# Attention over keys in multiples of 64, and top-k selection as two halves on 64 partitions

## What is computed

```python
# neighbourhood attention: grid of 8 rows x 64 columns, 8 heads of 64; the window is all 8 rows x 16 columns
col_idx = clip(cols - 8, 0, 48)[:, None] + arange(16)
s = einsum("bjhd,brjchd->bhjrc", q_i, k[..., col_idx]) + bias        # 128 keys of each query
p = softmax(s); o = einsum("bhjrc,brjchd->bjhd", p, v[..., col_idx])

# expert choice: each expert takes its top 64 of the group's 512 tokens
probs = softmax(h @ w_router)
gates, idx = top_k(probs.T, 64)
```

## Time and profile before

| what | us |
|---|---|
| median of three runs (2392.83 to 2403.08) | 2393.67 |
| the profiled execution | 2390.59 |
| its span, first to last instruction | 2388.9 |
| TensorE busy (15272 products) | 2250.4 (94%) |
| VectorE busy | 1564.9 (66%) |
| ScalarE busy | 1199.2 (50%) |
| GpSimd busy | 424.2 (18%) |
| attention stage | 773.8 to 1027 |
| output stage with the selection | 1027 to 1271 |
| expert stage | 1271 to 2389 |

### The profile page before, as it was taken

One profiled execution on the slowest core, in us unless ns is written; L12 is line 12 of the kernel. 1 busy time (PEld: TensorE's weight loads), 2 busy tenths in 40 slices (PEclk: granted clock), 3 DMA queues, 4 the chain that ended last, 5 costly groups with the idle time before them and its releaser, 6 DMA issues. The chain is left out here.

```text
span 2388.9 us, 39541 instructions
## 1 busy us (share of the span) xinstructions
PE 2250.4 (94%) x15272; PEld 1817.8 (76%) x15272; DVE 1564.9 (66%) x1802; ACT 1199.2 (50%) x1371; POOL 424.2 (18%) x380
## 2 busy tenths in 40 slices
PE   5999998988988999999976999999999999999997
PEld 3777787777776777777865888888888888888885
DVE  5556311555454444464438888889898888898987
ACT  5232222232231333352215777767777777777775
POOL 6111202232241100000421011111110111111101
PEclk9999999999997999999987999999999999999998
DMA  8445642010010323165347999999999999999997
GB/s 293 159 145 161 165 110 65 3 37 20 20 50 8 115 84 96 64 215 177 120 151 273 368 389 387 384 383 383 383 382 384 390 387 384 384 382 377 386 385 285
DMA packets 268466, 557.52 MB, mean 233 GB/s; under 512 B 13496, under 2 KB 66845, under 8 KB 265277
## 3 DMA queue, kind: packets, MB, share of 16 engines
q1 hardware_dynamic: 258989, 530.16, 61.4%
q0 software_dynamic: 4752, 17.30, 2.7%
q10 hardware_dynamic: 4608, 8.39, 0.9%
HBM read 511.73 MB, written 44.07 MB: 233 GB/s over the span
## 5 line engine op out<-in xcount | busy, mean ns | idle before, releaser
L2574 PE MATMUL ps<-whigh,xeT 128*128 128x512 f32 x2048 | 655.7, 394 | 1.5 <-DVE xeT L2746 1.5
L2754 DVE TENSOR_TENSOR wlow<-hT,whigh 128x2048 fp32r<-128x2048 f32 x192 | 432.1, 2285 | 62.8 <-ACT whigh L2678 62.8
L2574 PEld LDWEIGHTS ps<-whigh,xeT 128*128 128x128 f32 x2048 | 385.5, 188 | 80.4 <-issue 1.9
L2574 PE MATMUL ps<-wlow,xeT 128*128 128x512 f32 x1024 | 399.6, 390 | 0.0
L2678 ACT ACTIVATE whigh<-hT 128x2048 fp32r<-128x2048 f32 x192 | 358.7, 1911 | 10.2 <-PE ps L2574 10.2
L2574 PE MATMUL ps<-whigh,hidT 128*128 128x512 f32 x1024 | 327.8, 391 | 0.0
L2754 DVE TENSOR_TENSOR wlow<-oaT,whigh 128x2048 fp32r<-128x2048 f32 x96 | 216.8, 2287 | 41.3 <-ACT whigh L2678 41.3
L2754 DVE TENSOR_TENSOR wlow<-obT,whigh 128x2048 fp32r<-128x2048 f32 x96 | 217.9, 2285 | 21.1 <-ACT whigh L2678 21.1
L2574 PEld LDWEIGHTS ps<-whigh,hidT 128*128 128x128 f32 x1024 | 192.2, 188 | 40.3
L2574 PEld LDWEIGHTS ps<-wlow,xeT 128*128 128x128 f32 x1024 | 193.0, 188 | 38.0
L2678 ACT ACTIVATE whigh<-oaT 128x2048 fp32r<-128x2048 f32 x96 | 181.8, 1913 | 39.1 <-PEq L2561 21.8
(11 more groups left out here) (318 smaller groups left out, 3607.8 us busy)
## 6 DMA issues: line engine op xcount, KB each, us to landing
hT<-in_w_down SPq DMA_DIRECT2D x66, 1024.0 KB, 9.2
obT<-in_w_up SPq DMA_DIRECT2D x64, 1024.0 KB, 9.3
hT<-in_w_up SPq DMA_DIRECT2D x64, 1024.0 KB, 7.5
hT<-in_w_gate SPq DMA_DIRECT2D x62, 1024.0 KB, 9.8
oaT<-in_w_down SPq DMA_DIRECT2D x62, 1024.0 KB, 7.8
oaT<-in_w_gate SPq DMA_DIRECT2D x34, 1024.0 KB, 9.0
obT<-in_w_gate SPq DMA_DIRECT2D x32, 1024.0 KB, 6.9
oaT<-in_w_ada SPq DMA_DIRECT2D x20, 1024.0 KB, 7.6
```

Of the source, the lines that this page charges most:

```text
L2574: mm = pe.matmul(out, lhs[x], rhs[y], start=start and i == 0, stop=stop and i == 2)
L2754: dve.tensor_tensor(wlow[slot][:, :], raw[(FIRST + x) % RAW_SLOTS], whigh[slot][:, :].bitcast(F32), ALU.subtract).then_inc(low_done, 1)
```

## The change

The keys of a token tile are cut at multiples of 64 tokens, not 128: 192 keys for t = 0 and 3, 256 for t = 1 and 2. The probabilities are always transposed in two blocks of 128 columns; for 192 keys the second block begins at 64 and shares 64 columns with the first. So that every block meets its values, V's token tiles are shifted by 64: `vtok` has five tiles, the first with tokens 0 to 63 and zeros below, the last with zeros above and tokens 448 to 511. `load_v` puts the first and the last 64 tokens side by side with one DMA a group and the rest with a third; ScalarE copies `vtok` in three pieces; GpSimd zeroes the two halves once, ahead of the biases.

For the selection the 512 tokens of a group become two halves on 64 partitions (half, group, expert) by 256. Each half runs the eight rounds (the last without the replace), and then the two sorted lists of 64 are merged: value i of the first half against value 63-i of the second, the larger one is kept with its position. That gives the same 64 tokens in another order.

```diff
-KEY_TILES = [(0, 2), (0, 3), (1, 4), (2, 4)]
-BIAS_W = 896
+KEYS = [(0, 192), (64, 320), (192, 448), (320, 512)]
+BLOCKS = [(0, 64), (0, 128), (0, 128), (0, 64)]
+VALUE_TILES = [(0, 1), (1, 2), (2, 3), (3, 4)]
+BIAS_W = 640
...
 def load_v(eng, early_dram, first, h):
-    eng.dma_start(first["vT"], v[2, h]).then_inc(first["v_in"], 16)
+    src = v[2, h]
+    for g in range(GROUPS):
+        ends = src[:, g, :].rearrange("p (b c) -> p b c", c=CHUNK)[:, 0:NCHUNK:NCHUNK - 1, :]
+        eng.dma_start(first["vT"][:, g, 0:P].rearrange("p (b c) -> p b c", c=CHUNK), ends).then_inc(first["v_in"], 16)
+    eng.dma_start(first["vT"][:, :, P:], src[:, :, CHUNK:SEQ - CHUNK]).then_inc(first["v_in"], 16)
...
-    KINDS = [(16, 48), (0, 48), (0, 32)]
+    KINDS = [(16, 40), (8, 40), (8, 32)]
...
             def _(pool):
+                pool.memset(vtok[CHUNK:P, :, 0, :], 0.0).then_inc(v_zero, 1)
+                pool.wait_ge(v_zero, 1)
+                pool.memset(vtok[0:CHUNK, :, TPG, :], 0.0).then_inc(v_zero, 1)
+                pool.wait_ge(v_zero, 2)
                 for h in range(PAIRS):
...
                     if g == 0:
-                        pe.wait_ge(v_in, 16 * (h + 1))
+                        pe.wait_ge(v_in, 48 * (h + 1))
...
                     pe.matmul(ps[:, 2 + w % 2, 0:width(t)], qT[h % 2][rows, g, t * P:(t + 1) * P],
-                              kT[h % 2][rows, g, k0 * P:k1 * P], start=True, stop=True).then_inc(s_ps, 1)
+                              kT[h % 2][rows, g, k0:k1], start=True, stop=True).then_inc(s_ps, 1)
...
-                    for i in range(width(t) // P):
-                        mm = pe.transpose(ps[:, 4 + w % 2, i * P:(i + 1) * P], pr[:, w % 2, i * P:(i + 1) * P], ident)
+                    for i, at in enumerate(BLOCKS[t]):
+                        mm = pe.transpose(ps[:, 4 + w % 2, i * P:(i + 1) * P], pr[:, w % 2, at:at + P], ident)
...
-                    for i in range(k1 - k0):
+                    for i, tile in enumerate(VALUE_TILES[t]):
                         for hp in range(2):
                             rows = slice(hp * DH, (hp + 1) * DH)
-                            mm = pe.matmul(ps[rows, 6 + g, t * P:(t + 1) * P], vtok[:, g, k0 + i, rows],
-                                           pT[:, hp, i * P:(i + 1) * P], start=(i == 0), stop=(i == k1 - k0 - 1))
+                            mm = pe.matmul(ps[rows, 6 + g, t * P:(t + 1) * P], vtok[:, g, tile, rows],
+                                           pT[:, hp, i * P:(i + 1) * P], start=(i == 0), stop=(i == 1))
...
-                    act.activation(pT[:, v % 2, 0:width(t)], ps[:, 4 + v % 2, 0:width(t)], ACT.Copy).then_inc(pT_sb, 1)
+                    act.activation(pT[:, v % 2, :], ps[:, 4 + v % 2, 0:2 * P], ACT.Copy).then_inc(pT_sb, 1)
...
-                        act.activation(vtok[:, g, :, :], ps[:, 6 + g, :], ACT.Copy).then_inc(vtok_sb, 1)
+                        act.activation(vtok[0:CHUNK, g, 0, :], ps[0:CHUNK, 6 + g, 0:P], ACT.Copy)
+                        act.activation(vtok[CHUNK:P, g, TPG, :], ps[CHUNK:P, 6 + g, 0:P], ACT.Copy)
+                        act.activation(vtok[:, g, 1:TPG, :], ps[:, 6 + g, P:], ACT.Copy).then_inc(vtok_sb, 1)
...
-                for t in range(TPG):
-                    pe.wait_ge(probs_done, TPG + t + 1)
-                    mm = pe.transpose(ps[0:NR, 0, t * P:(t + 1) * P], probs[:, t, :, :].rearrange("p g e -> p (g e)"), ident)
+                for j in range(TPG // PARTS):
+                    pe.wait_ge(probs_done, NT - TPG // PARTS + j + 1)
+                    mm = pe.transpose(ps[0:PARTS * NR, 0, j * P:(j + 1) * P],
+                                      probs[:, j, :, :, :].rearrange("p h g e -> p (h g e)"), ident)
...
-                st.do(dve.tensor_copy(work[:, 0, :], ps[0:NR, 0, :]))
+                st.do(dve.tensor_copy(work[:, 0, :], ps[0:PARTS * NR, 0, 0:PLEN]))
                 for r in range(CAP // 8):
                     got = slice(8 * r, 8 * r + 8)
                     st.do(dve.max(vals[:, got], work[:, r % 2, :]))
                     st.did(dve.max_index(idx[:, got], vals[:, got], work[:, r % 2, :]))
-                    st.do(dve.match_replace(work[:, 1 - r % 2, :], vals[:, got], work[:, r % 2, :], -1.0))
-                dve.wait_ge(sel_const, 8)
-                st.do(dve.tensor_scalar(idxf, idx[:, :], first[:, 0:1], None, ALU.add))
-                st.did(dve.tensor_tensor(spread[:, 0, :, :], bcast(vals, 1, GROUPS), own[:, :, :], ALU.mult))
-                st.do(dve.tensor_tensor(spread[:, 1, :, :], bcast(idxf, 1, GROUPS), own[:, :, :], ALU.mult))
+                    if r < CAP // 8 - 1:
+                        st.do(dve.match_replace(work[:, 1 - r % 2, :], vals[:, got], work[:, r % 2, :], -1.0))
+                st.settle()
+                dve.wait_ge(sel_const, SEL_CONSTS)
+                st.did(dve.tensor_scalar(idxf, idx[:, :], first[:, 0:1], None, ALU.add))
+                st.do(dve.tensor_copy(other[0:NR, :], vals[NR:2 * NR, ::-1]))
+                st.did(dve.tensor_copy(otheri[0:NR, :], idxf[NR:2 * NR, ::-1]))
+                st.did(dve.tensor_tensor(ahead[0:NR, :], vals[0:NR, :], other[0:NR, :], ALU.is_ge))
+                st.do(dve.tensor_tensor(vals[0:NR, :], vals[0:NR, :], other[0:NR, :], ALU.max))
+                st.did(dve.tensor_tensor(diff[0:NR, :], idxf[0:NR, :], otheri[0:NR, :], ALU.subtract))
+                st.do(dve.tensor_tensor(spread[:, 0, :, :], bcast(vals[0:NR, :], 1, GROUPS), own[:, :, :], ALU.mult))
+                st.do(dve.tensor_tensor(chosen[0:NR, :], diff[0:NR, :], ahead[0:NR, :], ALU.mult))
+                st.do(dve.tensor_tensor(chosen[0:NR, :], chosen[0:NR, :], otheri[0:NR, :], ALU.add))
+                st.do(dve.tensor_tensor(spread[:, 1, :, :], bcast(chosen[0:NR, :], 1, GROUPS), own[:, :, :], ALU.mult))
```

## The result

The kernel after takes 2375.89 us (median of 5 executions, 2374.08 to 2377.34); the kernel before takes 2394.04 us (5 executions, 2392.83 to 2403.08). The ratio is 0.9921, 95% interval 0.9906 to 0.9936. The prediction was 2376.6 us, 17.1 us gained; the medians lie 18.15 us apart. A second measurement of the same two kernels, in the experiments, gave 2374.67 against 2393.18 us, ratio 0.9921 (0.9908 to 0.9935).

The account below looks back on a forecast made before the run. The prediction took attention to be bound by TensorE's instructions and selection by VectorE latency: 11.7 + 5.4 = 17.1 us off a median of 2393.7 gives 2376.6 us, ratio 0.9929, range 2371 to 2385 us.

Parts of the forecast that it names:

- What bounds each stage: Attention bound by TensorE's own instructions; selection by latency of VectorE's small instructions, TensorE waiting 18.8 us.
- Scores: Attention: 384 to 256 keys gains 3.4 us, 256 to 192 gains 1.7 (bounds 0 and 1.7), less 0.1.
- Values and transposes: Attention, tiles 1 and 2: fewer value products gain 3.5 us, fewer transposes 3.2 us.
- the prediction's sign: What the profile after should show: attention taking 241.5 us instead of 253.2, with no new TensorE wait.
- ScalarE's three copies: Attention: vtok copied in three pieces, 0.60 us each if full price; hidden, cost nothing, 9.6 us at worst.
- V's load: Attention, SyncE's queue: three DMAs ahead of the gate weights cost nothing, bounds 0 and 1 us.
- GpSimd's memsets: Attention: two memsets ahead of bias take 0.8 us with their waits, but cost nothing on the path.
- Selection: Copy to pick: 6.4 us from halved length, 0.65 from the dropped replace, less 1.6 for the merge; 5.4 gained.
- The door: Expert stage's start: selection gain taken whole, 6 us of cover; the rival, gain lost there, 2382.0 us, chance 0.07.
- Rival 3: Attention and expert stage starts: clock rises at another moment by chance, 4 us shifting 2 us; over 2 us, chance 0.10.
- Rival 4: Attention: clock falls to 1.2 GHz; 35 us there cancels everything, 60 us gives 2407 us; chance 0.05.
- The total: Whole kernel: 17.1 us gained, median 2376.6 us, ratio 0.9929; faster by over 0.5%, chance 0.80.

Follow-up runs that it names:

- pe_work_back: Kernel after, with TensorE given back its old attention work (wider scores, third transpose and third value products, results unread); 2390.57 us in one execution, beside 2394.87 of before.
- scores_256: Kernel after, with the 192-key attention scores widened to 256 keys; 2376.60 us in one execution, slot 1 to slot 32 1.61 us longer.
- two_rounds: Kernel after, with two of the selection's eight rounds and fixed token positions, so the choice of tokens is left out; 2364.43 us.
- warm_tight: Kernel after plus idle TensorE products, 52 of 128x512 during the selection and 18 small ones during the gather; median 2372.43 us, again 2372.16.
- warm_experts: Kernel after plus idle TensorE products, 30 during the selection and 40 small ones during the gather; 2376.56 us, ratio 0.9934 to before.

## Why the prediction was right, and where it was not

- **What bounds each stage**: right. In the stretch from slot 1 to slot 32 the gain was TensorE's instructions to the last hundredth (`pe_work_back`), and the selection's was latency.
- **Scores**: 3.4 and 1.7 us predicted; `scores_256` measured 1.6 for the 1.7. **Values and transposes**: no experiment took them apart, but the rows of after agree for the values, with 0.59 us (924.48 to 925.07) in the slots where 12 records had cost 0.81; for the transposes six records cost 0.63 us to the next start and four 0.41, so 3.5 us rather than 3.2 by that reading. The sum was 11.7 and came out as 11.46. The whole of attention shrank by more than the prediction's sign, 253.2 to 241.5 us: from the first scores to the last values it is 238.1 us instead of 251.5, 13.4 less, by the first slot.
- **ScalarE's three copies**: they take 0.27, 0.27 and 0.49 us, not 0.6 each, and cost nothing. **V's load**: no wait. The rule that spoke against it (the Trainium skill, DMA: Bandwidth & Descriptors, section Specifications: 512 B at least for full rate) would, at the price that the prediction gave it, have brought the weights some 4 us late. They landed 4.8 us after their issue instead of 5.6, with V's pieces of 256 B in front, and 1.7 us ahead of the split; with pieces of 64 B the wait was 1.59 us. A cost of that size did not show here.
- **GpSimd's memsets**: "nothing" is the step that did not hold. Not as a cost, though: VectorE's waits for bias stand at 2.1 us for both heads, before at 2.0. Together with the narrower biases the memsets changed which bias VectorE's first split met, and with the new attention the first slot became 1.8 us shorter. The prediction looked at who waits for the memsets and not at what they push aside. That the 1.8 us come by this path is the likeliest reading, not a shown one.
- **Selection**: a MAX8 of 256 takes 0.42 us, as the slope said (0.68 - 0.266 = 0.41), the 64 partitions added nothing to that, and the ten instructions with the pick behind them took 2.37 us (1249.70 to 1252.07) for 2.4. The sum of 5.4 was measured as 5.44. **The door**: taken whole, and `two_rounds` shows that it would have been for more than twice as much.
- **Rival 3**: its size was right (4 us of rise for 2 us of time), its nature wrong. The shifts of -1.8 and about +1 us repeat with the code. They partly cancel, and that the total was hit this closely is in part luck. From the Trainium skill's statement that the monitor's window runs free of the kernel (TensorE: Matmul & The Clock Gate, section What's actually happening) I had concluded that shifts come by chance. The conclusion is not what the fourteen traces show: among kernels with the same code ahead of the restart the rise moves by less than 0.5 us against attention's first scores, while these move by 4.8 against the start of the trace (773.87 to 778.65). The statement itself is not refuted by that. At attention the kernel and the clock's rise keep step; how they come to do so, no run here shows.
- **Rival 4**, a fall of the clock in attention: 1.00 in after, as in before.
- **The total**: 17.1 us predicted, 11.46 + 5.44 = 16.9 by the two mechanisms, 1.8 - 1.1 us more by the clock, 17.6; the medians say 18.15 and the interval leaves 15.3 to 22.5, so the totals tell neither 17.1 from 17.6 nor the terms apart. The profiled executions differ by 15.4, mostly since attention began 1.7 us later in that of after.

## What to carry to other kernels

Where one engine never waits, the distance to the next start of its own instructions, read in a trace at two sizes, prices a third size to a tenth of a microsecond. Where a chain of small instructions is the path, count the instructions and take the fixed part and the slope of each: on twice the partitions with half the length, a round went from 2.155 to 1.36 us and not to half, since the fixed parts stay. At a restart behind idle time, look also at what an added instruction pushes aside on the engines around it; a third of a microsecond there went along with 1.5 more by the clock, and the same shift came back in every run of that code.

## What I had not expected of the hardware

- The clock's rise is repeatable: the first product wholly at full speed came 4.7 to 5.1 us after attention's first scores in twelve traces, 8.4 and 8.5 in two; the clock rose 8.8 to 9.1 us after the first tokens in seven, 7.0 and 7.1 in two.
- A TensorE that is kept at work does not stay at full clock in every case. In `warm_tight` the small products, 1.2 us behind the pick, ran through these stretches (columns as in rows 2):

```profile
1252.00:1254.00 2.00, 1.72 (x13) 1.75 (x14) 0.00 (x0) 1.83 (x2) 1.04 (x2) 0.86 0.00 0
1254.00:1256.00 2.00, 2.00 (x11) 2.00 (x11) 1.89 (x1) 2.00 (x3) 0.36 (x1) 0.50 0.42 90
1256.00:1258.00 2.00, 2.00 (x17) 2.00 (x16) 2.00 (x2) 1.68 (x1) 0.00 (x0) 0.79 0.62 203
```

  The clock fell to 0.50 behind the short idle times around the pick (0.23 and 1.21 us) and was back at 1.00 in time for the tokens. The small fp32 products took 0.14 us a record in `warm_experts` (11.12 us, 80 records) and 0.16 here (5.88 us, 36 records), over stretches that were partly at 1.2 GHz, so few of them fill a gap.
- Strided DMAs into SBUF of 64 B pieces: 96 KB landed in 4.0 us, and four of them in a row kept the issuing queue for 4.34 us. The weights behind them were issued 3.1 us later than in after, counted from attention's first scores, and landed 3.5 us later: the issuing queue, more than the landing, set the delay.
